# A decoder step on one core: expert turns dealt anew between the stages of a tile pair, and where their v rows are added up

## The chip, the cores and the metric

One core of a Trainium2 chip runs the whole kernel. The metric is device microseconds (us) of one execution. The engines are TensorE (PE in the profile, with its weight loads as PEld), VectorE (DVE), ScalarE (ACT), GpSimd (POOL) and SyncE (SP, which only issues transfers). Each engine runs its own program in order; they meet through semaphores.

## What is computed

One layer of a hybrid decoder over 1024 prompt tokens (8 tiles of 128 rows) and 8 sample tokens with a paged cache of 4096 positions each. Every token goes through latent attention and retention side by side, merged by sigmoid gates, and then through a product-key expert layer. Cut to what matters here:

```python
def merge_branches(o_lat, o_ret, rg, ga, gb, w_uv, ret_norm_g, w_oa, w_ob, w_out):
    o_a = einsum('bshc,chv->bshv', o_lat, w_uv).reshape(B, S, -1) @ w_oa
    o_b = (silu(rg) * head_group_norm(o_ret, ret_norm_g)) @ w_ob
    return (sigmoid(ga) * o_a + sigmoid(gb) * o_b) @ w_out

def peer_block(tb, w_q, sub_keys, expert_u, expert_v):      # 128 tokens
    q = rms(tb @ w_q)                                        # 8 heads x 2 halves x 128
    s = einsum('thpd,phkd->thpk', q, sub_keys)               # 128 keys per half
    sv, si = top_k(s, 16)
    eid, g = best 16 of the 16 x 16 sums, softmax of them    # per head
    act = gelu(einsum('thk d,td->thk', expert_u[eid], tb))
    return einsum('thk,thkd->td', g * act, expert_v[eid])
```

The expert layer dominates the traffic: each token picks 8 x 16 = 128 experts, and for each of these one row of 1024 floats is read from `expert_u` and one from `expert_v`. For one tile that is 128 u gathers and 128 v gathers, each of 128 partitions x 4 KB = 524,288 bytes.

## The kernel before

**Two strands.** The *front* of a tile is everything up to the choice of its experts; the *experts* are the gathers and what is done with them. The front of later tiles is computed while the experts of earlier tiles run. The experts are written as steps (L2498 on VectorE, L1339 on TensorE, L2603 on ScalarE): step s takes u row s (one VectorE instruction, L2507, a product with the token and a sum, into `dots`) and v row s - 20 (`LAG`). There are 8 x 128 + 20 = 1044 steps, and two steps make a *turn* (522 turns). GpSimd (L814) issues all gathers in that order, u and v by turns, into a ring of 9 row buffers (`RING`); a buffer comes free when its row is used.

**Where a v row is added up.** Either VectorE multiplies it by its coefficient and adds it into `xr` (L2535), or TensorE multiplies it by a diagonal of coefficients and adds it into PSUM (L1351: two matmuls of 128x512 floats, which the profile has as four records; ScalarE makes the diagonal first, L2629, three steps ahead, in 8 slots). The list `on_pe` (L504 to L507) says which: it looks up the name of the stage in which step n + 20 runs. Stages in `ALL_ON_PE` give all their v rows to TensorE, those in `MOST_ON_PE` two of three, those in `HALF_ON_PE` every second one, and all others none.

**Units.** The tiles go in five units: (0), (1, 2), (3, 4), (5, 6), (7). A unit of two, a pair, does attention and retention of its two tiles one after the other (the *tile stages*: lat, uq, reto, squares, normed, keys, 16 of head, ov for each), then the *output stages* for both at once, so that each weight block is read once and used for both: rg (8 loads), oa (4), gate (8), ob (8), gate (8), merge, out (8), x2, wq (16). A load is 512 KB into one of 4 slots of `wbuf`, issued by SyncE as slots come free; for a pair it feeds four matmuls of 128x512 (eight records). Last comes *choosing*: pqT (2), top (4), xT, linA (24 loads, which are the first weight blocks of the next lead tile and of the tile beside it) on TensorE, while VectorE picks the best keys and works out the ids (`choose` L2156, `dve_chosen` L2200). After the five units comes the sample part, with the paged cache.

**How the order is set.** Each engine's front is a generator that yields the name of its stage; all three yield the same names in the same order. `beside` (L843) takes the front up to a yield, then lets the experts run as many turns as the deal gives to that place, on each of the three engines:

```python
def dealt(names, total, weight):                       # L481
    for i, n in enumerate(names):
        so_far += weight(i, n)
        upto = int(total * so_far / whole + 0.5)
        deal.append(upto - given)
```

`total` is the unit's number of turns, `UNIT_TURNS` = (0, 64, 128, 128, 72), and the weights are `BESIDE` (L2709). The sample part has the other 130 turns, by `SAMPLE_SHARES`.

**Draining.** TensorE writes a block into one of four PSUM banks in turn (`A`, banks 0, 1, 2, 6); for a pair, two banks per block. ScalarE drains it (`act_block`, L1427): it yields once less than the block has loads, waits until the block is used up (`w_used`), drains both banks, then yields once more. `act_linA` (L1475) has the same form with 3 + 1 yields. On VectorE, `gated` and `gate` (L2054, L2073) apply the gates; where they stand among the yields is written out at L2097 to L2130. TensorE may refill a bank only after it was drained (`may_fill`), so a block waits for the drain of the one two before it.

Of the kernel before, what the change touches and what calls it, by code (L numbers as in the profile page):

```python
# [107 lines left out]
def program(nc, a, out, const):  # L108
    _, SEQ, D = a["x_prompt"].shape
    NB = a["x_sample"].shape[0]  # L110
    _, NPHYS, PAGE, KVL = a["cache_ckv"].shape
    ROPE = a["cache_krope"].shape[3]
    _, _, RH, RDK, RDV = a["state_ret"].shape
# [5 lines left out]
    _, _, PH, NK, PD = a["peer_sub_keys"].shape  # L119
# [73 lines left out]
    with ExitStack() as ctx:  # L193
# [1233 lines left out]
        def act_block(act, tiles, name, i, emit, ready=None):  # L1427

            for _ in range(load_at[tiles[0], name, i][1] - 1):
                yield name  # L1430
            if ready is not None:
                ready()
            act.wait_ge(w_used, used_through(tiles[0], name, i))
            for x, t in enumerate(tiles):
                emit(x, A.bank(t, name, i)).then_inc(A.drained, 1)
            yield name
# [38 lines left out]
        def act_linA(act, t):  # L1475
# [17 lines left out]
            for i in range(NA):  # L1493
                for _ in range(3):
                    yield "linA"
# [8 lines left out]
                yield "linA"  # L1504
# [543 lines left out]
        def dve_unit(dve, u):  # L2048
# [47 lines left out]
            for i in range(4):  # L2096
                yield "rg"  # L2097
            for x in range(2):
                gated(0, x)
                yield "rg"  # L2100
            yield "rg"
            yield "rg"
            for x in range(2):
                gated(1, x)
                yield "oa"
            yield "oa"
            yield "oa"
            for i in range(4):
                yield "gate"
# [3 lines left out]
            yield "gate"  # L2113
            yield "gate"
            for x in range(2):
                gate(1, x)
                yield "ob"
            for i in range(6):
                yield "ob"
            for i in range(4):  # L2120
                yield "gate"
# [3 lines left out]
            yield "gate"  # L2125
            yield "gate"
# [550 lines left out]
        def _(dve):  # L2677
# [31 lines left out]
BESIDE = {"lat": 1.5, "uq": 1.0, "reto": 1.5, "squares": 1.5, "normed": 1.5, "keys": 1.5, "head": 2.0, "ov": 1.5, "rg": 0.25, "oa": 0.25,  # L2709
          "gate": 0.25, "ob": 0.25, "merge": 2.0, "out": 0.25, "x2": 2.0, "wq": 0.3, "pqT": 1.0, "top": 1.0, "xT": 1.0, "linA": 0.4,  # L2710
          "end": 0.0}
ALL_ON_PE = ("lat", "uq", "reto", "squares", "normed", "keys", "ov", "merge", "x2", "pqT", "top", "xT")
MOST_ON_PE = ("head", "page")
HALF_ON_PE = ("ret",)
# [70 lines left out]
```

## Time and profile before

| | |
|---|---|
| runs of the kernel before | 4503.61 and 4514.61 us, median 4509.11 us |
| the profiled execution, its own time | 4466.19 us |
| its span | 4464.4 us |
| HBM read | 1404.99 MB |
| row gathers (software queue q0) | 1082.26 MB |
| mean granted TensorE clock | 0.871 |
| 1024 u gathers, 1024 v gathers on GpSimd | 1129.5 and 1242.3 us busy |
| VectorE: 1024 u rows (L2507), 422 v rows (L2535) | 1239.2 and 542.8 us busy |
| TensorE: 602 v rows (L1351, 2408 records) | 1320.7 us busy |

The profiled execution is one of its own, 42.9 us (1%) below the median of the runs. Busy time of TensorE is modelled: back to back, a record of 128x512 begins every 0.43 us, though its mean length is given as 0.6. GB/s in a window is all traffic of the core, and "DMA share" is how busy its 16 DMA engines were.

### The profile page before, as it was taken

Reading aid. Unit: us, or ns where it says so; the run is one execution under the profiler, and the core shown is the slowest. Engines: PE = TensorE matmul, PEld = TensorE weight load, DVE = VectorE, ACT = ScalarE, POOL = GpSimd, SP = SyncE. Lnnn points to the kernel's source line nnn. Section 1 sums busy time; section 2 is a strip of 40 time slices with the busy share of each in tenths; the row PEclk is TensorE's granted clock in tenths of the full one; section 3 lists DMA queues with packets and bytes.
Section 4 is the critical chain, followed back from the end, with each engine's and each line's share of the span. In section 5 each row is a group of like instructions: output and inputs, shape, how many; then the busy total and the mean of one; then the engine's idle time right before and its main releaser. Section 6 shows DMA issues by size and latency. Waiting matters only on the chain.

```text
span 4464.4 us, 38637 instructions
## 1 busy us (share of the span) xinstructions
PE 3261.3 (73%) x11093; PEld 1612.4 (36%) x11093; DVE 2729.5 (61%) x6242; ACT 725.0 (16%) x2211; POOL 2390.5 (54%) x2069
## 2 busy tenths in 40 slices
PE   7886889887686898866776988677773667778313
PEld 4343434433232344333333444233331335545211
DVE  2157633686666536976656446976548757676676
ACT  2112210211121112111121112121111111111101
POOL 0006732347777533557767434557536656566774
PEclk8997899998898999978898999888897789988556
DMA  5758986679999987989999977889998999999996
GB/s 172 242 187 307 357 289 220 237 256 375 363 379 363 358 283 274 330 294 349 365 371 356 334 270 278 323 320 350 371 350 303 327 346 345 369 364 350 393 398 256
DMA packets 541606, 1425.12 MB, mean 319 GB/s; under 512 B 88234, under 2 KB 147251, under 8 KB 541395
## 3 DMA queue, kind: packets, MB, share of 16 engines
q0 software_dynamic: 297216, 1082.26, 65.3%
q1 hardware_dynamic: 197666, 314.45, 20.5%
q10 hardware_dynamic: 46514, 25.96, 2.0%
q8 instruction: 90, 1.47, 0.1%
q14 instruction: 120, 0.98, 0.1%
HBM read 1404.99 MB, written 17.47 MB: 319 GB/s over the span
## 4 chain that ended last, share of the span: by engine, by line
PE 32%; POOL 20%; DVE 17%; issue 15%; DMA 11%; another core or an unknown queue 2%; ACT 2%; SPq 0%; ACTq 0%; DVEq 0%; POOLq 0%
POOL rows L820 20%; PE PS L884 18%; DMA rows<-in_peer_v_dram,pe_id 6%; PE PS L1351 6%; DVE rows L2507 3%; DVE xr L2535 3%; PE PS L941 2%; PE PS L864 1%; DMA out_ret_s_dram<-KV 1%; DMA rows<-in_peer_u_dram,pe_id 1%; DVE WK L2248 1%; DMA wbuf<-in_w_in_dram 1%; PE PS L1268 1%; DVE WK L2251 1%
## 5 line engine op out<-in xcount | busy, mean ns | idle before, releaser
L820 POOL DMA_INDIRECT rows<-in_peer_v_dram,pe_id x1024 | 1242.3, 1213 | 1182.9 <-DVE dots L2507 899.0
L1351 PE MATMUL PS<-rows,diags 128*128 128x512 f32 x2408 | 1320.7, 688 | 472.3 <-DMA rows<-in_peer_v_dram,pe_id 414.9
L2507 DVE CUSTOM_DVE_ANT_0 rows<-rows,px 128x1024 f32<-128x1024 f32 x1024 | 1239.2, 1221 | 573.2 <-DMA rows<-in_peer_u_dram,pe_id 528.8
L820 POOL DMA_INDIRECT rows<-in_peer_u_dram,pe_id x1024 | 1129.5, 1103 | 837.3 <-DVE pe_id L2255 290.8
L1351 PEld LDWEIGHTS PS<-rows,diags 128*128 128x128 f32 x2408 | 487.1, 217 | 1130.4 <-issue 1104.2
L2535 DVE SCALAR_TENSOR_TENSOR xr<-rows,gcoef,xr 128x1024 f32<-128x1024 f32 x422 | 542.8, 1286 | 89.0 <-issue 72.0
L884 PE MATMUL PS<-wbuf,xt 128*128 128x512 f32 x800 | 400.1, 609 | 30.0 <-DMA wbuf<-in_peer_w_q_dram 11.9
L884 PE MATMUL PS<-wbuf,z 128*128 128x512 f32 x752 | 384.9, 596 | 4.6 <-DMA wbuf<-in_w_oa_dram 2.6
L2629 ACT ACTIVATE diags<-ident,gcoef 128x128 f32<-128x128 f32 x602 | 209.7, 393 | 296.6 <-DVE gcoef L2524 143.4
L941 PE MATMUL PS<-wbuf,xt 128*128 128x512 f32 (+1 forms) x480 | 226.3, 569 | 22.3 <-DMA wbuf<-in_w_in_dram 9.8
L884 PE MATMUL PS<-wbuf,wide 128*128 128x512 f32 (+1 forms) x416 | 204.1, 602 | 33.1 <-ACT z L1451 10.4
L884 PEld LDWEIGHTS PS<-wbuf,xt 128*128 128x128 f32 x800 | 149.9, 194 | 213.1 <-issue 170.0
L884 PEld LDWEIGHTS PS<-wbuf,z 128*128 128x128 f32 x752 | 143.7, 191 | 187.6 <-issue 177.5
L864 PE MATMUL PS<-ident,WK 128*128 128x128 f32 x548 | 92.6, 313 | 145.0 <-DVE WK L2296 46.6
L864 PE MATMUL PS<-ident,z 128*128 128x128 f32 x133 | 24.5, 323 | 181.8 <-DVE z L1954 176.2
L864 PEld LDWEIGHTS PS<-ident,WK 128*128 128x128 f32 x548 | 78.6, 165 | 199.7 <-issue 51.5
L949 PE MATMUL PS<-wbuf,KV 128*128 128x512 f32 (+1 forms) x288 | 135.1, 551 | 0.0
L941 PEld LDWEIGHTS PS<-wbuf,xt 128*128 128x128 f32 x480 | 86.5, 194 | 117.2 <-issue 79.1
L884 PEld LDWEIGHTS PS<-wbuf,wide 128*128 128x128 f32 x416 | 80.1, 198 | 134.9 <-issue 89.5
L1024 PE MATMUL PS<-KV,qt 96*128 96x512 f32 (+3 forms) x192 | 89.6, 582 | 44.2 <-DVE mx L2032 32.5
L1045 PE MATMUL PS<-KV,WK 128*128 128x64 f32 x576 | 85.1, 296 | 47.5 <-issue 28.7
L1574 ACT ACTIVATE WK<-PS 128x512 f32<-128x512 f32 (+3 forms) x96 | 44.1, 489 | 400.3 <-PE PS L864 267.7
(417 smaller groups left out, 2937.0 us busy)
## 6 DMA issues: line engine op xcount, KB each, us to landing
wbuf<-in_w_in_dram SPq DMA_DIRECT2D x226, 512.0 KB
wbuf<-in_peer_w_q_dram SPq DMA_DIRECT2D x88, 512.0 KB
wbuf<-in_w_out_dram SPq DMA_DIRECT2D x44, 512.0 KB
wbuf<-in_w_ob_dram SPq DMA_DIRECT2D x42, 512.0 KB
KV<-in_cache_ckv_dram SPq DMA_DIRECT2D x144, 128.0 KB
rows<-in_peer_u_dram,pe_id POOLq DMA_INDIRECT x1028, 5.4
rows<-in_peer_v_dram,pe_id POOLq DMA_INDIRECT x1024
wbuf<-in_w_oa_dram SPq DMA_DIRECT2D x24, 512.0 KB
```

The lines of the kernel that those rows point to most:

```text
L820: pool.indirect_dma_start(row_slot(kind, n), None, a["peer_u" if kind == "u" else "peer_v"][0], bass.IndirectOffsetOnAxis(ap=pe_id[t % 3][ ...
L864: last = nc.tensor.transpose(b[0:m, k * n:(k + 1) * n], src, ident[0:n, 0:n])
L884: last = nc.tensor.matmul(b[:, 0:wd], lhs[x][:, (k0 + j) * P:(k0 + j + 1) * P], block_w[:, j * wd:(j + 1) * wd], start=(k0 + j == 0), stop ...
L941: last = nc.tensor.matmul(A.bank(t, "linA", i)[:, 0:wd], xt[:, (k0 + j) * P:(k0 + j + 1) * P], block_w[:, j * wd:(j + 1) * wd], start=(fir ...
L949: last = nc.tensor.matmul(other[:, 0:wd], next_lhs(t, k0 + j), block_w[:, j * wd:(j + 1) * wd], start=(first_k and j == 0), stop=(last_k a ...
L1024: last = nc.tensor.matmul(DJ.bank(t, "score", h)[:, i:i + w], qt[0:HD, h * P:(h + 1) * P], key_t[0:HD, h, i:i + w], start=True, stop=True)
L1045: last = nc.tensor.matmul(bank[6][:, h * VH:(h + 1) * VH], pt[:, k * P:(k + 1) * P], value[:, k, h * VH:(h + 1) * VH], start=(k == 0), sto ...
L1268: last = nc.tensor.matmul(PS[:, at_:at_ + P], qsc[b % 2][:, k * P:(k + 1) * P] if k < 8 else qsc_rope[b % 2], blocks_of[:, k] if k < 8 els ...
L1351: last = nc.tensor.matmul(bank[3 + 4 * c], diag(n), row_slot("v", n)[:, c * 512:(c + 1) * 512], start=start, stop=stop)
L2507: V.tensor_tensor_reduce(out=row, in0=row, in1=px[:, :], scale=1.0, scalar=0.0, op0=ALU.mult, op1=ALU.add, accum_out=dots[:, at_:at_ + 1]) ...
L2535: V.scalar_tensor_tensor(out=y[:, :], in0=row_slot("v", n), scalar=gcoef[:, g % 2 * TOPK + k:g % 2 * TOPK + k + 1], in1=y[:, :], op0=ALU.m ...
L2629: nc.scalar.activation(diag(n), ident[:, :], ACT.Copy, scale=gcoef[:, g % 2 * TOPK + k:g % 2 * TOPK + k + 1]).then_inc(diag_ready.sem, 1)
```

## The change

The turns stay the same in number for every unit (`UNIT_TURNS` is not touched), and the sample part keeps its deal. What changes is the split inside a unit, the engine of some v rows, and the place of some drains and gates:

1. New weights in `BESIDE`: less for the tile stages, more for the output stages and for pqT and top.
2. linA joins `ALL_ON_PE`; head moves from `MOST_ON_PE` (two of three v rows on TensorE) to `HALF_ON_PE`.
3. `act_block` and `act_linA` drain a block one yield later, that is, behind the turns dealt to the block's last load.
4. On VectorE `gated` and `gate` stand later by up to four yields, to match.

```diff
@@ act_block
-            for _ in range(load_at[tiles[0], name, i][1] - 1):
+            for _ in range(load_at[tiles[0], name, i][1]):
                 yield name
             if ready is not None:
                 ready()
             act.wait_ge(w_used, used_through(tiles[0], name, i))
             for x, t in enumerate(tiles):
                 emit(x, A.bank(t, name, i)).then_inc(A.drained, 1)
-            yield name
@@ act_linA
-                for _ in range(3):
+                for _ in range(4):
                     yield "linA"
...
-                yield "linA"
@@ dve_unit
-            for i in range(4):
+            for i in range(8):
                 yield "rg"
-            for x in range(2):
-                gated(0, x)
-                yield "rg"
-            yield "rg"
-            yield "rg"
-            for x in range(2):
-                gated(1, x)
-                yield "oa"
-            yield "oa"
-            yield "oa"
-            for i in range(4):
+            for i in range(2):
+                for x in range(2):
+                    gated(i, x)
+                    yield "oa"
+            for i in range(6):
                 yield "gate"
             for x in range(2):
                 gate(0, x)
                 yield "gate"
-            yield "gate"
-            yield "gate"
+            for i in range(2):
+                yield "ob"
             for x in range(2):
                 gate(1, x)
                 yield "ob"
+            for i in range(4):
+                yield "ob"
             for i in range(6):
-                yield "ob"
-            for i in range(4):
                 yield "gate"
             for x in range(2):
                 gate(2, x)
                 yield "gate"
-            yield "gate"
-            yield "gate"
@@ the tables
-BESIDE = {"lat": 1.5, "uq": 1.0, "reto": 1.5, "squares": 1.5, "normed": 1.5, "keys": 1.5, "head": 2.0, "ov": 1.5, "rg": 0.25, "oa": 0.25,
-          "gate": 0.25, "ob": 0.25, "merge": 2.0, "out": 0.25, "x2": 2.0, "wq": 0.3, "pqT": 1.0, "top": 1.0, "xT": 1.0, "linA": 0.4,
+BESIDE = {"lat": 1.0, "uq": 0.8, "reto": 1.2, "squares": 1.2, "normed": 1.2, "keys": 1.2, "head": 1.5, "ov": 1.0, "rg": 0.45, "oa": 0.45,
+          "gate": 0.45, "ob": 0.45, "merge": 2.5, "out": 0.5, "x2": 2.5, "wq": 0.45, "pqT": 2.0, "top": 1.5, "xT": 1.0, "linA": 0.45,
           "end": 0.0}
-ALL_ON_PE = ("lat", "uq", "reto", "squares", "normed", "keys", "ov", "merge", "x2", "pqT", "top", "xT")
-MOST_ON_PE = ("head", "page")
-HALF_ON_PE = ("ret",)
+ALL_ON_PE = ("lat", "uq", "reto", "squares", "normed", "keys", "ov", "merge", "x2", "pqT", "top", "xT", "linA")
+MOST_ON_PE = ("page",)
+HALF_ON_PE = ("ret", "head")
```

## Rows read from the trace of the kernel before

**Rows 1.** The page: busy time of each engine, then 40 slices.

```profile
PE 3261.3 (73%) x11093; PEld 1612.4 (36%) x11093; DVE 2729.5 (61%) x6242; ACT 725.0 (16%) x2211; POOL 2390.5 (54%) x2069
...
PE   7886889887686898866776988677773667778313
...
POOL 0006732347777533557767434557536656566774
...
DMA  5758986679999987989999977889998999999996
```

**Rows 2.** Busy time by window, stages in turn; the first line names columns.

```profile
core 0: us, PE busy (x) PEld busy (x) DVE busy (x) ACT busy (x) POOL busy (x), PEclk, DMA share, GB/s
340.30:593.00 252.70, 188.17 (x527) 96.16 (x528) 171.72 (x367) 61.55 (x180) 181.13 (x156) 0.84 0.93 340
593.00:842.20 249.20, 234.92 (x619) 109.76 (x618) 87.31 (x228) 40.18 (x122) 54.01 (x46) 0.98 0.69 236
842.20:970.30 128.10, 94.89 (x264) 46.81 (x263) 122.97 (x451) 19.03 (x61) 42.47 (x34) 0.88 0.69 237
970.30:1503.00 532.70, 386.98 (x986) 176.87 (x987) 332.93 (x641) 95.96 (x279) 396.92 (x355) 0.89 0.97 364
1503.00:1776.00 273.00, 249.82 (x645) 116.80 (x644) 128.79 (x284) 42.46 (x130) 102.98 (x90) 0.96 0.83 295
1776.00:1939.10 163.10, 109.79 (x295) 50.67 (x293) 156.43 (x504) 21.53 (x70) 81.89 (x68) 0.87 0.83 295
...
2919.60:3159.80 240.20, 186.27 (x556) 92.85 (x557) 152.07 (x285) 50.00 (x131) 167.62 (x156) 0.90 0.95 353
3159.80:3361.50 201.70, 149.20 (x353) 63.19 (x352) 99.09 (x209) 26.80 (x83) 84.99 (x73) 0.92 0.96 359
3361.50:3472.90 111.40, 26.63 (x60) 10.24 (x58) 99.80 (x274) 10.37 (x29) 73.38 (x60) 0.65 0.81 286
```

**Rows 3.** Waits in the second pair's tile stages (total, times, longest).

```profile
DVE rows L2507 <- DMA rows<-in_peer_u_dram,pe_id: 161.0, 117, 3.3
PE PS L1351 <- DMA rows<-in_peer_v_dram,pe_id: 107.6, 57, 5.2
```

**Rows 4.** Chain of waits, second pair's output stages: start, us, what.

```profile
1503.51 68.68 PE PS L884 x160
...
1577.47 56.91 PE PS L884 x128
...
1640.12 6.87 PE PS L1351 x16
```

**Rows 5.** VectorE's groups, 1829 to 1939 us, second pair's choosing.

```profile
L2535 DVE SCALAR_TENSOR_TENSOR xr<-rows,gcoef,xr 128x1024 f32<-128x1024 f32 x20 | 25.8, 1289 | 0.7 <-issue 0.6
L2507 DVE CUSTOM_DVE_ANT_0 rows<-rows,px 128x1024 f32<-128x1024 f32 x20 | 24.5, 1224 | 0.3
```

**Rows 6.** Busy time by window, choosing stages of two pairs (columns as before).

```profile
841.60:875.00 33.40, 20.54 (x74) 11.80 (x72) 31.34 (x154) 11.85 (x44) 12.53 (x11) 0.85 0.55 182
...
949.40:979.80 30.40, 9.95 (x27) 5.05 (x26) 29.26 (x64) 3.04 (x10) 11.81 (x8) 0.66 0.52 158
1775.30:1826.40 51.10, 34.30 (x106) 15.95 (x105) 48.18 (x213) 14.36 (x52) 26.16 (x22) 0.93 0.75 258
1826.40:1905.90 79.50, 76.18 (x193) 35.18 (x191) 76.88 (x237) 6.01 (x13) 45.18 (x38) 0.98 0.98 361
1905.90:1948.90 43.00, 9.67 (x23) 4.78 (x23) 41.69 (x82) 3.82 (x13) 16.35 (x13) 0.56 0.62 203
```

**Rows 7.** Weight-load waits of TensorE, second pair's choosing.

```profile
PEld PS L864 <- DVE z L1954: 33.7, 1, 33.7
```

**Rows 8.** GpSimd's groups, 1826.4 to 1934.5 us, second pair's choosing.

```profile
L820 POOL DMA_INDIRECT rows<-in_peer_v_dram,pe_id x23 | 31.7, 1376 | 44.0 <-DVE dots L2507 38.9 <-issue 5.1
```

**Rows 9.** GpSimd's groups, 1042.8 to 1237.6 us, heads of one tile.

```profile
L820 POOL DMA_INDIRECT rows<-in_peer_v_dram,pe_id x67 | 79.9, 1193 | 20.7 <-issue 20.1 <-DVE dots L2507 0.6
```

**Rows 10.** Waits in the second pair's output stages.

```profile
ACT WK L1421 <- PE PS L884: 87.5, 7, 23.1
```

## The prediction

> **What bounds the kernel now.** I read the page first, for which engine is full. None is: TensorE is busy for 73% of the span, the others less, but the DMA line stands at 9 in long stretches and falls to 7 or 8 between them, and there GpSimd falls to 3 or 4 [rows 1]. So the limit changes with the stage, and I cut the span into windows at each unit's stages [rows 2]: for each unit tile stages, output stages (rg to wq), choosing (pqT to linA). The reader is to see three patterns in the second pair. Tile stages: 532.7 us, DMA share 0.97, 364 GB/s, no engine over 75%. Output stages: 273.0 us, TensorE busy 249.8, DMA only 0.83 and 295 GB/s. Choosing: 163.1 us, VectorE busy 156.4, DMA again 0.83. The waits agree: in the tile stages VectorE and TensorE wait for rows to arrive, 161.0 and 107.6 us [rows 3]; in the output stages the chain is unbroken runs of weight matmuls, 160 records in 68.68 us [rows 4]. The rows are thus short of bandwidth in one stage while bandwidth lies idle in the two others.
>
> The deal before, by the formula: a pair's weights sum to 128.4, of which the two tiles have 90, so of 128 turns 90 lie in the tile stages, 21 in the output stages, 17 in choosing. After: 68 of 124.7, so 70, 36 and 22. The pair with 64 turns goes from 45, 11, 8 to 35, 18, 11; the single tile with 72 from 40, 17, 15 to 28, 26, 18. A turn moves four rows, 2.10 MB, which is 5.76 us at 364 GB/s.
>
> **Fewer turns in the tile stages.** They are bound by arriving rows, so a turn gone is its transfer gone: 20 x 5.76 = 115 us in the second pair, and the same in the third. The last tile: 12 turns at 353 GB/s, 5.94 us each, 71. The first pair's share is 0.93, not 0.97, so I take 50 of the 58 that 10 turns give. Sum -351. What is late next must stay below the rows: with half of the head rows on VectorE, a head turn costs it 2 x 1.22 + 1 x 1.29 = 3.7 us [rows 5] of 5.76, so VectorE is no bound; TensorE gets less work.
>
> **More turns in the output stages.** The second pair's output stages move 273 x 295 = 80.5 MB; 15 turns add 31.5. 112 MB at 361 GB/s (the rate of a window where TensorE runs at full pace, [rows 6]) is 310 us, 37 more than now. VectorE has room (128.8 of 273, plus some 65). TensorE gets one turn more at merge and one more at x2, 4 rows x 1.72 us (16 records took 6.87 us, [rows 4]) = 7 us, and it stands still while those rows arrive; since the bandwidth is counted already, I add only 3. So +40 for each of the two full pairs. Bounds: 7 us (all rows fit beside the matmuls) and 15 x 5.76 = 86 (nothing does). The first pair moves 58.8 + 14.7 MB, 204 us at 361, below its 249: +2. The last tile's output stages are at 0.96 already, so 9 turns cost 9 x 5.84 (359 GB/s) = +53. Sum +135.
>
> **Choosing.** Between the last wq block and linA TensorE needs 33.4 us with 3 turns and 51.1 with 7 [rows 6], 4.4 us a turn; 4 more make +18 in a full pair, 2 more +9 in the first. In linA, v rows leave VectorE: 20 x 1.289 = 25.8 us of the 109.8 in which it is nearly always busy [rows 5]. But what goes off it comes on TensorE: 76.2 us of linA matmuls [rows 6] and 22 rows x 1.72 = 38. Behind them stands what lies between choosing and the next tile's first block: of the 43.0 us there, 33.7 are TensorE's wait for the next tile's latents [rows 7], and 9 are left; I add 5 for making the latents and 3 for late rows. That is 131 us, against 79.5 + 43.0 = 122.5 now. VectorE was the bound; TensorE becomes it. So +9, not a gain, together +27 for a full pair (bounds: -10, if only VectorE's relief counts, and +50, if each of 5 more turns and each row waits for itself). First pair: 74.4 + 12 x 1.72 + 14 = 109 against 104.8, +4, so +13. The last tile has no linA matmuls, so its relief is real (VectorE 99.8 busy of 111.4, 20.7 off, 7.3 on), but 38 MB of traffic needs 106 us: -3. Sum 54 + 13 - 3 = +64.
>
> **Later drains and gates.** ScalarE now serves the turns behind a block's last load before it waits for that block, instead of waiting first. Queued behind its wait were diagonals and the tanh of the experts; they come sooner. What waits now is the bank: TensorE needs it for the block after next, 32 records or 13.75 us later. As long as ScalarE trails by less than that, the price is nothing; if it trails, it is one turn per block that has a turn behind it (below). A gain is bounded by gaps such as the 5.3 us between the two long matmul runs, 1572.2 to 1577.5 [rows 4]. I take 0. SyncE's and GpSimd's queues keep their order; only the turns between which weights are asked for differ.
>
> **Sum.** -351 + 135 + 64 = -152 us on the profiled execution's own 4466.2, which makes 4314. That execution lies 1% under the median of the runs, so the median comes to 4314 x 4509.1 / 4466.2 = 4356 us.
>
> A v gather takes GpSimd 1376 ns beside the full VectorE of choosing and 1193 ns in the heads [rows 8, 9], so something of VectorE's work may reach it; the v rows on VectorE go from 422 to 458. The Trainium skill, "SBUF — State Buffer", section "SBUF: two separate sides", has a rule against such a move: a VectorE instruction with two SBUF inputs and a GpSimd operation that reads SBUF hold one port pair in turn, each for its whole length. By that rule in full the gathers would wait for every added row, which is rival (d); the sum takes nothing for it.
>
> **Rivals.**
> (a) *All bandwidth gets used.* If every stage reached 364 GB/s, the second pair's 322.5 MB would take 886 us instead of 968.8 (-83), the third's the same, the last tile's 189 MB 520 instead of 553 (-33), and the first pair -50: -249, own time 4217, median 4258. For it: 361 GB/s beside full-pace matmuls [rows 6]. Against it: turns bunched at merge, x2, pqT and top, where TensorE stops.
> (b) *A moved turn costs its full price.* Output stages stretch by 5.76 us for every turn, as they would if blocks and rows can't overlap: 86 instead of 40 in each full pair, 40 instead of 2 in the first: -22 in all, 4444, median 4487. For it: the last tile's output stages are DMA-bound [rows 2]. Against it: in the full pairs 160 records hold 0.43 us each [rows 4] with 5 turns beside them, and the DMA share leaves 0.14 free.
> (c) *The drain falls behind and TensorE pays.* Its place is the bank wait before the next block but one; it decides once ScalarE trails TensorE by more than 13.75 us, because its tanh waits for a VectorE that waits for rows. Price on top of (b): 16 turns on 36 loads put one behind 4 to 5 of 10 blocks, 5.76 us each, 26 a full pair, 13 and 21 in the others, 86; and in linA matmuls and rows in series, 79.5 + 63 + 14 = 157 instead of 131 (+52 for two pairs, +14 in the first). -22 + 152 = +130, own 4596, median 4640: slower. For it: ScalarE's work is strictly in order, and rows arrive late where DMA is full. Against it: ScalarE now waits for TensorE (87.5 us in 7 waits, [rows 10]), so it has time in hand.
> (d) *VectorE's rows hold up the gathers.* 36 more rows x 1.289 = 46 us, all of it on the path: 4360, median 4403. Against it: GpSimd is busy for 397 of 533 us even in the tile stages [rows 2]. The rule of the Trainium skill quoted above would have it so for each of them.
>
> **Chances.** Forecast 0.50, (a) 0.14, (b) 0.19, (c) 0.10, (d) 0.07. The range is 4270 to 4480: it holds the forecast with most of its bounds (40 may be 7 or 60), (d), and parts of (a) and (b), and leaves (c) out. A change of 2%, 90 us, is about what a measurement of this kernel can tell; the line is at 4419. Faster by more: 0.45 from the forecast, 0.14, 0.05 from (d), 0.03 from (b), 0.67. Slower by more: most of (c), 0.08. Within: 0.25.
>
> **What would show it.** Right: the second pair's tile stages near 418 us, still at a DMA share of 0.96 or more; its output stages near 313 us at over 350 GB/s, with gaps between L884 runs; in choosing, TensorE busy for nearly all of linA, no L2535 there, and no wait of 30 us for the next tile's latents. The count of L2535 is 458, of L1351 2264. Wrong: tile stages that shrink by less than 4 us a turn with the DMA share falling (then the front, not the rows, sets them); output stages over 345 us, (b); waits of L884 for ScalarE over a few us each, (c); output stages at 273 us, more than half of (a).

## The result and the profile after

| | before | after |
|---|---|---|
| median of the runs, us | 4509.11 | 4259.67 (4254.52 to 4264.82) |
| ratio, 95% interval | 1 | 0.9447 [0.9377, 0.9517] |
| profiled execution, own time, us | 4466.19 | 4254.52 |
| its span, us | 4464.4 | 4252.7 |

The kernel became 5.5% faster. The forecast was 4356 us in a range of 4270 to 4480: the sign was right, the saving came out 96 us too small, and the measured time lies just below the range. Rival (a), in which every stage uses the bandwidth, had 4258.

The page of the changed kernel, to be laid beside [rows 1]: busy time, the DMA engines in 40 slices, and the two groups of v rows.

```profile
PE 3223.9 (76%) x10949; PEld 1589.4 (37%) x10949; DVE 2778.4 (65%) x6278; ACT 716.3 (17%) x2175; POOL 2441.1 (57%) x2069
...
DMA  5766987779999999999999999999999999999996
GB/s 176 232 209 238 346 308 271 261 256 351 372 372 360 402 370 342 330 326 364 364 376 372 376 374 325 330 367 376 390 358 349 352 331 367 353 365 361 401 402 228
...
L1351 PE MATMUL PS<-rows,diags 128*128 128x512 f32 x2264 | 1269.6, 700 | 450.7 <-DMA rows<-in_peer_v_dram,pe_id 393.9
...
L2525 DVE SCALAR_TENSOR_TENSOR xr<-rows,gcoef,xr 128x1024 f32<-128x1024 f32 x458 | 588.5, 1285 | 145.6 <-issue 119.8
```

The counts 2264 and 458 are those that the prediction named, so the deal came out as worked out there. (VectorE's lines stand 10 lower now: v rows L2525, dots L2497.) The DMA line no longer falls to 7 and 8 behind the first pair: it is 9 until the last slice. What the digits hide is in the line under it: the rate still swings from 325 to 402 GB/s while the digit stays 9.

The windows by stage, as [rows 2]: first pair (tile stages, output stages), second pair (tile, output, choosing), last tile (the same three). The ends of stages in this and later tables were read to within some 4 us.

```profile
341.20:553.00 211.80, 158.19 (x446) 86.81 (x447) 150.89 (x328) 55.03 (x159) 136.43 (x118) 0.76 0.87 318
553.00:807.30 254.30, 234.53 (x619) 109.42 (x618) 116.80 (x267) 40.28 (x123) 85.01 (x72) 0.97 0.79 280
951.60:1370.50 418.90, 302.36 (x793) 145.55 (x794) 285.50 (x534) 80.88 (x228) 303.41 (x276) 0.81 0.96 360
1370.50:1656.70 286.20, 263.60 (x663) 117.77 (x662) 199.16 (x382) 43.07 (x133) 192.89 (x142) 0.96 1.01 383
1656.70:1851.70 195.00, 164.18 (x414) 73.21 (x412) 153.37 (x528) 31.93 (x103) 109.00 (x96) 0.96 0.88 314
2744.60:2912.90 168.30, 135.89 (x447) 72.67 (x448) 122.74 (x232) 41.92 (x104) 120.17 (x108) 0.88 0.97 360
2912.90:3145.80 232.90, 159.91 (x353) 65.03 (x351) 144.09 (x268) 27.60 (x85) 139.88 (x109) 0.91 1.01 389
3145.80:3257.60 111.80, 73.23 (x152) 26.74 (x150) 88.94 (x274) 18.02 (x50) 86.88 (x70) 0.91 0.89 323
```

Subtracting [rows 2], and doing the same for the third pair (420.5, 287.8 and 184.6 us now, against 542.3, 274.0 and 164.2), gives every term of the sum. All in us of the profiled executions.

| term | forecast | measured |
|---|---|---|
| tile stages (first, second, third pair, last tile) | -50, -115, -115, -71 = -351 | -41, -114, -122, -72 = -348 |
| output stages | +2, +40, +40, +53 = +135 | +5, +13, +14, +31 = +64 |
| choosing | +13, +27, +27, -3 = +64 | +16, +32, +20, 0 = +69 |
| start and sample part | 0 | +5 |
| sum | -152 | -212 |

One term is off, by half: the output stages. The sum of -212 is also somewhat small beside the medians, which differ by 249: before's profiled execution lay 1% under its runs' median, the changed kernel's only 0.1% under its own. The forecast carried before's 1% over to the changed kernel. So of the 96 us that it missed, 60 lie in the sum, and 36 in this step from the profiled execution to the median. The ratio is the better measure, and two more chips gave 0.9439 and 0.9438 (below).

A closer look at the second pair, windows again: a stretch of output stages between two waits, then from the last wq block to linA, linA, and from there to the next tile's first block.

```profile
1372.00:1510.00 138.00, 132.14 (x301) 54.77 (x300) 95.67 (x139) 16.91 (x43) 97.86 (x68) 0.98 1.04 401
1655.80:1736.40 80.60, 54.18 (x139) 22.52 (x138) 69.75 (x265) 20.09 (x70) 55.59 (x48) 0.92 0.87 310
1736.40:1846.70 110.30, 110.30 (x278) 50.99 (x277) 81.01 (x246) 11.35 (x31) 53.12 (x47) 1.00 0.89 312
1846.70:1861.00 14.30, 9.81 (x27) 4.63 (x26) 12.68 (x38) 3.05 (x10) 5.70 (x7) 0.88 1.00 357
```

In the first line TensorE is busy for 96% of the time and the DMA engines move 401 GB/s beside it. The prediction had 361 GB/s as the ceiling [rows 6]. The page of the kernel before already had two slices above that, 393 and 398 GB/s in the sample part, where weight loads run beside the rows (the third and second from the end):

```profile
GB/s 172 242 187 307 357 289 220 237 256 375 363 379 363 358 283 274 330 294 349 365 371 356 334 270 278 323 320 350 371 350 303 327 346 345 369 364 350 393 398 256
```

In the third line of the windows TensorE is busy all the time and VectorE is not: linA's bound has passed from the one to the other, as forecast.

The chain of waits of the second pair's output stages, which was unbroken matmuls before [rows 4]:

```profile
1371.15 24.26 PE PS L884 x56
1395.42 11.27 DMA wbuf<-in_w_oa_dram
...
1414.19 12.58 DMA wbuf<-in_w_in_dram
```

And the waits of the same stretch (total, times, longest):

```profile
ACT WK L1421 <- PE PS L884: 86.9, 7, 16.8
POOL rows L820 <- DVE dots L2497: 49.4, 8, 18.6
...
PEld PS L884 <- DMA wbuf<-in_w_in_dram: 17.0, 18, 2.2
```

Some weight loads now land late, by 2.2 us at most and 17.0 us in all for the loads of `w_in`, where the stage before had no such wait; part of this is hidden behind running matmuls. The chain draws such a load at its full length of 11 us, though TensorE stood still for 1.4 us at most. TensorE's busy time in this stage by line, v rows (L1351) before and after, then the blocks (L884) before and after:

```profile
1503.00:1776.00 273.00, 25.93 (x50) 10.46 (x48) 0.96 0.83 295
1370.50:1656.70 286.20, 33.23 (x66) 13.35 (x64) 0.96 1.01 383
...
1503.00:1776.00 273.00, 210.92 (x480) 90.60 (x480) 0.96 0.83 295
1370.50:1656.70 286.20, 217.77 (x480) 89.35 (x480) 0.96 1.01 383
```

The stage grew by 13.2 us. The four more v rows on TensorE took 7.3 us, which the prediction had priced at 7, though its sum took only 3. The same 480 records of the blocks took 6.9 us more: about what the traffic of 15 turns cost them. ScalarE waits for TensorE as before [rows 10], so it has not fallen behind.

### The profile page after: what moved, and what is told of

Read it like the earlier page. It is cut to its first block, busy times and chain, and to the rows that moved or that the text cites. A ratio compares the mean times of both kernels' runs of the same rounds, so it can differ in the third digit from the quotient of the medians.

```text
span 4252.7 us, 38318 instructions
## 1 busy us (share of the span) xinstructions
PE 3223.9 (76%) x10949; PEld 1589.4 (37%) x10949; DVE 2778.4 (65%) x6278; ACT 716.3 (17%) x2175; POOL 2441.1 (57%) x2069
## 4 chain that ended last, share of the span: by engine, by line
PE 39%; DMA 17%; POOL 17%; issue 12%; DVE 10%; ACT 3%; another core or an unknown queue 2%; ACTq 0%; SPq 0%; DVEq 0%; POOLq 0%
POOL rows L820 17%; PE PS L884 15%; PE PS L1351 10%; DMA rows<-in_peer_v_dram,pe_id 8%; PE PS L941 4%; DMA wbuf<-in_w_in_dram 4%; DVE rows L2497 3%; PE PS L949 2%; PE PS L864 1%; DMA wbuf<-in_peer_w_q_dram 1%; DMA rows<-in_peer_u_dram,pe_id 1%; DVE xr L2525 1%; DMA out_ret_s_dram<-KV 1%; PE PS L1268 1%
## 5 line engine op out<-in xcount | busy, mean ns | idle before, releaser
L820 POOL DMA_INDIRECT rows<-in_peer_v_dram,pe_id x1024 | 1256.2, 1227 | 845.2 <-DVE dots L2497 554.1
L820 POOL DMA_INDIRECT rows<-in_peer_u_dram,pe_id x1024 | 1165.6, 1138 | 912.9 <-DVE pe_id L2245 291.7
L1351 PE MATMUL PS<-rows,diags 128*128 128x512 f32 x2264 | 1269.6, 700 | 450.7 <-DMA rows<-in_peer_v_dram,pe_id 393.9
L2497 DVE CUSTOM_DVE_ANT_0 rows<-rows,px 128x1024 f32<-128x1024 f32 x1024 | 1237.9, 1221 | 453.5 <-DMA rows<-in_peer_u_dram,pe_id 396.5
L1351 PEld LDWEIGHTS PS<-rows,diags 128*128 128x128 f32 x2264 | 460.0, 218 | 1064.4 <-issue 1014.9
L2525 DVE SCALAR_TENSOR_TENSOR xr<-rows,gcoef,xr 128x1024 f32<-128x1024 f32 x458 | 588.5, 1285 | 145.6 <-issue 119.8
L884 PE MATMUL PS<-wbuf,xt 128*128 128x512 f32 x800 | 409.0, 618 | 53.5 <-DMA wbuf<-in_w_in_dram 29.7
L884 PE MATMUL PS<-wbuf,z 128*128 128x512 f32 x752 | 386.3, 598 | 7.5 <-DMA wbuf<-in_w_oa_dram 5.7
L2619 ACT ACTIVATE diags<-ident,gcoef 128x128 f32<-128x128 f32 x566 | 200.8, 395 | 312.8 <-DVE gcoef L2514 153.1
L884 PEld LDWEIGHTS PS<-wbuf,xt 128*128 128x128 f32 x800 | 147.3, 195 | 253.2 <-issue 144.5
L884 PE MATMUL PS<-wbuf,wide 128*128 128x512 f32 (+1 forms) x416 | 204.3, 604 | 32.2 <-ACT z L1450 10.4
L884 PEld LDWEIGHTS PS<-wbuf,z 128*128 128x128 f32 x752 | 144.2, 192 | 192.4 <-issue 178.4
L949 PE MATMUL PS<-wbuf,KV 128*128 128x512 f32 (+1 forms) x288 | 134.5, 549 | 0.0
L884 PEld LDWEIGHTS PS<-wbuf,wide 128*128 128x128 f32 x416 | 80.0, 198 | 132.6 <-issue 85.5
L1045 PEld LDWEIGHTS PS<-KV,WK 128*128 128x128 f32 x576 | 79.5, 214 | 53.9 <-issue 27.3
```

The source lines that it names most:

```text
L820: pool.indirect_dma_start(row_slot(kind, n), None, a["peer_u" if kind == "u" else "peer_v"][0], bass.IndirectOffsetOnAxis(ap=pe_id[t % 3][ ...
L884: last = nc.tensor.matmul(b[:, 0:wd], lhs[x][:, (k0 + j) * P:(k0 + j + 1) * P], block_w[:, j * wd:(j + 1) * wd], start=(k0 + j == 0), stop ...
L949: last = nc.tensor.matmul(other[:, 0:wd], next_lhs(t, k0 + j), block_w[:, j * wd:(j + 1) * wd], start=(first_k and j == 0), stop=(last_k a ...
L1045: last = nc.tensor.matmul(bank[6][:, h * VH:(h + 1) * VH], pt[:, k * P:(k + 1) * P], value[:, k, h * VH:(h + 1) * VH], start=(k == 0), sto ...
L1351: last = nc.tensor.matmul(bank[3 + 4 * c], diag(n), row_slot("v", n)[:, c * 512:(c + 1) * 512], start=start, stop=stop)
L2497: V.tensor_tensor_reduce(out=row, in0=row, in1=px[:, :], scale=1.0, scalar=0.0, op0=ALU.mult, op1=ALU.add, accum_out=dots[:, at_:at_ + 1]) ...
```

## The experiments

Each ratio is to the kernel before, run on the same chip. Chips differ (the kernel before took 4420 to 4482 us on them), so ratios of different chips are compared with care, and medians not at all.

### The parts alone (one chip, kernel before 4476.86 us)

**Only the deal**: `BESIDE` of the changed kernel, everything else as before.

> The kernel before with only the new weights of the deal; v rows stay where they were (two of three head rows on TensorE, linA rows on VectorE), drains and gates stand where they stood. Theory T (the gain is bandwidth that lay idle in the output stages and is now used by moved turns): nearly all of the gain, 0.950 to 0.962 of the kernel before, second pair's tile stages near 420 us, its output stages at over 375 GB/s and under 292 us. Rival D (the later drains and gates are what lets the turns ride along): output stages over 310 us, ratio 0.975 or more. Rival V (the engine of the v rows matters as much): ratio 0.97 or more, with choosing the stage that is longer.

**Only the later drains and gates**: the three hunks in `act_block`, linA's drain and the gates.

> The kernel before with only the drains and gates one turn further on. Theory T: 0.997 to 1.003 of the kernel before. Rival D: 0.99 or less, from shorter output stages (under 268 us in the second pair).

**Only the lists of v rows**:

```diff
-ALL_ON_PE = (..., "xT")
-MOST_ON_PE = ("head", "page")
-HALF_ON_PE = ("ret",)
+ALL_ON_PE = (..., "xT", "linA")
+MOST_ON_PE = ("page",)
+HALF_ON_PE = ("ret", "head")
```

> The kernel before with only the new lists of stages: linA rows all on TensorE, head rows split evenly. Theory T: within 0.994 to 1.004 of the kernel before; linA goes from 109.8 us, bound by VectorE, to 105 to 112, bound by TensorE; the tile stages stay at 530 us, since arriving rows set them. Rival V: 0.985 or less.

**The changed kernel with the drains and gates of before**:

> The changed kernel with drains and gates back in their old places. Theory T: within 0.5% of the changed kernel, so 0.944 to 0.955 of the kernel before. Rival D: 0.97 or more, with ScalarE waiting for TensorE ahead of the turns' diagonals and output stages over 300 us in the second pair.

| | median, us | ratio |
|---|---|---|
| only the deal | 4288.49 | 0.9573 [0.9543, 0.9602] |
| only drains and gates | 4484.06 | 1.0013 [0.9995, 1.0032] |
| only the lists | 4449.09 | 0.9931 [0.9910, 0.9952] |
| changed, old drains | 4252.09 | 0.9493 [0.9466, 0.9520] |

The deal brings 4.3%, the lists 0.7% alone and 0.8% on top of the deal, the drains alone nothing. (The last row leaves the changed kernel's ratio, 0.944 to 0.945 on three other chips, by 0.5%; a comparison on one chip follows below.) The deal's own windows (second pair's tile, output and choosing stages, last tile's choosing):

```profile
943.00:1368.40 425.40, 311.24 (x861) 151.61 (x862) 264.29 (x517) 86.26 (x245) 318.13 (x276) 0.88 0.95 355
1368.40:1655.50 287.10, 262.44 (x663) 117.84 (x662) 197.14 (x382) 42.99 (x133) 177.70 (x142) 0.96 1.00 383
1655.50:1852.30 196.80, 129.80 (x326) 56.70 (x324) 179.52 (x550) 25.24 (x81) 114.72 (x96) 0.87 0.88 315
...
3155.00:3289.50 134.50, 37.80 (x92) 15.16 (x92) 112.93 (x306) 15.55 (x47) 87.88 (x72) 0.70 0.82 297
```

The output stages are at 383 GB/s here too, so neither the lists nor the drains made that rate. Against the run with only the drains, on the same chip, the deal takes 367 us from the tile stages and adds 60 to the output stages and 91 to choosing. That last number is 31 more than in the changed kernel with old drains on the same chip: with linA's v rows on VectorE, it is busy for 179.5 of 196.8 us, and the last tile's choosing takes 134.5 us instead of 116.2. The lists give that back. In the run of the lists alone the second pair's choosing, and the last tile's, are

```profile
1783.80:1948.70 164.90, 144.03 (x374) 65.92 (x372) 132.56 (x484) 27.58 (x90) 79.71 (x68) 0.95 0.83 290
...
3360.90:3464.90 104.00, 63.19 (x140) 23.65 (x140) 85.40 (x284) 19.77 (x58) 72.63 (x61) 0.94 0.87 316
```

against 164.2 and 119.2 us in the run of the drains alone: nothing in the second pair, where TensorE takes over as the bound, and 15 us in the last tile, which has no linA matmuls. The third pair's choosing became 10 us shorter (154.6 against 164.9), which the second pair's did not.

### The engines of the v rows, and the number of row buffers (another chip, kernel before 4419.92 us)

**The changed kernel once more**, as the measure for the next three:

> The changed kernel itself, as the measure of the other runs of this group. Both theories: 0.948 to 0.951 of the kernel before.

**Head rows two thirds on TensorE again**: "head" back in `MOST_ON_PE`.

> The changed kernel with the head rows two of three on TensorE again (linA rows stay on TensorE). Theory T (heads are bound by arriving rows whichever engine adds them up): within 0.3% of the changed kernel, tile stages of the second pair 415 to 425 us. Rival V (the even split relieves TensorE on the path): 0.5 to 1% slower than the changed kernel.

**linA's rows split evenly**: "linA" from `ALL_ON_PE` to `HALF_ON_PE`.

> The changed kernel with every second linA row on VectorE again. Theory T (TensorE alone sets linA now, 110.3 of 110.3 us busy, with 19 us in rows that could go to VectorE at 81 of 110): linA in the second pair 94 to 100 us, the whole 0.5 to 1% faster than the changed kernel. Rival: VectorE's order of work holds it (its ids must be ready first), linA at 105 us or more and no gain.

**One row buffer fewer**: `RING = 8` instead of 9.

> The changed kernel with 8 row buffers instead of 9. Theory E (the DMA engines are full in the tile stages): tile stages of the second pair longer by under 2%, 360 GB/s kept. Rival Q (the ring of buffers, so the number of rows under way, limits the tile stages, and this is why they stop at 360 GB/s when the output stages reach 383): tile stages longer by 5 to 12%, under 345 GB/s.

| | median, us | ratio |
|---|---|---|
| changed kernel | 4173.04 | 0.9439 [0.9403, 0.9476] |
| head rows mostly on TensorE | 4193.37 | 0.9492 [0.9453, 0.9530] |
| linA's rows split | 4162.48 | 0.9398 [0.9362, 0.9434] |
| 8 buffers (one round) | 4269.48 | 0.9650 [0.9598, 0.9703] |

Taking head rows off VectorE again made the kernel 0.5% slower by the medians, and not faster: rival (d) is wrong. The intervals of the ratios overlap, but the fastest of its four runs (4189.12 us) is above the slowest of the changed kernel's four (4185.05). The prediction had given the even split nothing. Where the gain lies is not shown: the second pair's tile stages took 414.4 us here against 403.5, but 414.7 with linA's rows split, where the heads are as in the changed kernel:

```profile
936.20:1350.90 414.70, 299.12 (x792) 144.43 (x793) 285.87 (x534) 80.32 (x228) 307.06 (x276) 0.81 0.97 363
```

So this stage differs by 11 us between executions without any change to its own turns. Splitting linA's rows shortened the two full pairs' choosing by 11 and 5 us and the first pair's by 10, and cost the last tile 6. In the whole time that is 0.25% by the medians and 0.4% by the ratios, with runs and intervals that overlap, where 0.5 to 1% was expected: no gain is shown for the kernel. In the stage itself both extremes are too much for linA in a pair, a bound on VectorE and one on TensorE.

With 8 buffers the second pair's tile and output stages are

```profile
959.20:1385.20 426.00, 303.56 (x793) 146.80 (x794) 285.72 (x534) 80.36 (x228) 308.39 (x277) 0.82 0.95 355
1385.20:1672.20 287.00, 260.88 (x662) 116.70 (x661) 198.98 (x382) 43.11 (x133) 190.40 (x141) 0.98 1.00 380
```

and with 9, on the same chip,

```profile
944.00:1347.50 403.50, 296.94 (x791) 143.32 (x792) 285.13 (x534) 80.33 (x228) 293.84 (x276) 0.82 0.98 374
1347.50:1635.00 287.50, 263.61 (x665) 117.74 (x664) 198.61 (x382) 43.08 (x133) 171.93 (x142) 0.97 1.00 382
```

The tile stages lose 22 us, the output stages none. Since the second pair's tile stages vary by 11 us, the third pair's are the better witness: 426.9 us with 8 buffers, 405.4, 406.8 and 407.4 in the three kernels with 9. The rate of the tile stages therefore depends on how many rows are under way, and is no ceiling of the memory, although the DMA share stands at 0.95 to 0.98 beside it. It isn't set by the buffers alone: 11% fewer of them took 4 to 5% off the rate, to 355 and 360 GB/s in the two pairs, where the theory of the buffers had expected under 345.

### Weight loads beside rows where there were none (one look)

If rows alone can't fill the DMA engines, loads in another queue should raise the traffic. This kernel issues 24 extra loads of weights during the heads of each unit's last tile (six rounds over the first four weight buffers, which nobody reads until the real loads):

```diff
+            for rep in range(6):
+                for n in range(first, first + WSLOTS):
...
+                    sp.dma_start(w_place(n)..., w[...]).then_inc(again, 16)
```

> The changed kernel with 24 more weight loads of 512 KB (12.6 MB) in each unit, issued by SyncE into the four weight slots before the first real rg loads, two and two, while the heads of the unit's last tile run; they hold the same data as the real ones. Theory Q (the DMA engines have time left when only row gathers are under way, and transfers of another queue use it): in the second pair's last 26 head turns, now about 54 MB in 150 us or 360 GB/s, the traffic rises to 380 GB/s or more, and those heads take 165 to 175 us. Theory E (360 to 374 GB/s is what the core can read in that stage): GB/s stays within 2% of the stage without the loads and the heads take 185 us.

Its one execution took 4348.88 us, beside 4481.48 for the kernel before. The extra loads, in the timeline:

```profile
1232.31 86.76 SPq L685 DMA_DIRECT2D wbuf<-in_w_in_dram  x24
```

Windows in the heads of the same pair without them, with them, and behind them, then all of the 26 head turns:

```profile
1059.00:1145.00 86.00, 57.10 (x130) 26.34 (x130) 59.42 (x99) 14.58 (x38) 62.50 (x60) 0.74 0.96 365
1232.00:1333.00 101.00, 57.31 (x146) 26.70 (x145) 52.15 (x90) 14.98 (x38) 60.66 (x54) 0.76 1.03 400
1340.00:1420.00 80.00, 50.07 (x132) 23.70 (x133) 50.74 (x82) 10.53 (x29) 55.97 (x52) 0.83 0.99 370
1243.10:1420.00 176.90, 105.03 (x260) 49.09 (x261) 104.58 (x169) 22.30 (x62) 114.37 (x101) 0.78 1.01 387
```

365, 400, 370 GB/s: the traffic rises by 8 to 10% with the second queue and falls when it ends. (The last four loads of the unit are issued at 1333 us; behind them, from 1380 us, it is 343 GB/s.) It is not free for the rows: 12.6 of the 40.4 MB in the middle window are weights, so rows came at 275 GB/s there. The 26 head turns took 176.9 us, where the changed kernel has 153.7 at 364 GB/s, on another chip. The 12.6 MB would be 35 us at that rate and cost 23. That lies between the two theories: the rate of 387 passes the 380 of the one, the time misses its 165 to 175 us by 2.

### How far the deal can go

**More turns still in the output stages**:

```diff
-BESIDE = {... "head": 1.5,  ... "rg": 0.45, "oa": 0.45, "gate": 0.45, "ob": 0.45, ... "out": 0.5,  ...
+BESIDE = {... "head": 1.27, ... "rg": 0.65, "oa": 0.65, "gate": 0.65, "ob": 0.65, ... "out": 0.65, ...
```

That makes 62, 44 and 22 turns of a pair instead of 70, 36 and 22.

> The changed kernel with the deal pushed on: 8 more turns of a full pair from the heads (70 to 62) into the output stages (36 to 44). Theory T: the output stages are full at 383 GB/s now, so (109.6 + 16.8) MB need 330 us instead of 286, as much as the tile stages give back (46 us): within 0.5% of the changed kernel, 0.940 to 0.950 of the kernel before. Rival (turns still ride for about 1 us each as the first 15 did): output stages under 300 us, ratio 0.93 or less.

**More turns in linA, split evenly**: linA 0.7, pqT 1.5, top 1.2, the blocks 0.5.

> The changed kernel with every second linA row on VectorE and the deal moved once more: in a full pair 3 turns fewer in the tile stages and 3 fewer between wq and linA, 6 more in linA. Theory T (each stage at its own bound): between wq and linA 58 to 63 us instead of 77, linA 105 to 115 instead of 92, tile stages 17 us shorter; 0.930 to 0.938 of the kernel before. Rival (VectorE holds linA, since choosing the ids is its own work): linA over 125 us, ratio 0.94 or more.

On one chip (kernel before 4481.48 us): 4204.96 us, 0.9381 [0.9353, 0.9409], and 4242.47 us, 0.9453 [0.9421, 0.9486]. The first is a small gain over the changed kernel's 0.944 of other chips, the second none, although 0.930 to 0.938 was expected of it. In the first the pairs' output stages (first pair, second pair) read

```profile
517.90:777.90 260.00, 239.34 (x621) 110.97 (x620) 141.85 (x303) 40.90 (x125) 108.26 (x92) 0.96 0.87 316
...
1292.10:1618.50 326.40, 258.54 (x655) 117.29 (x654) 240.74 (x437) 42.71 (x132) 225.81 (x173) 0.91 1.01 390
```

Against the changed kernel's 286 to 289 us on three other chips, 8 more turns cost the second pair some 39 (330 us was expected), 5 each: this stage is full near 390 GB/s, and past it a turn pays nearly its price. That is the mean of a flat stretch and a slower one; four windows of 40 us from its start read 400, 402, 404 and 402 GB/s. In the first pair 4 more turns cost nothing; there was still room, at 316 GB/s.

The second kernel shows that the count of turns isn't all. It has 36 turns in the output stages of a pair, as the changed kernel has, and yet they took 303.3 and 302.9 us. The second pair's, in two parts, and then the changed kernel's:

```profile
1341.30:1500.00 158.70, 147.80 (x346) 63.14 (x346) 111.24 (x163) 21.40 (x52) 112.64 (x81) 0.98 1.03 401
1500.00:1644.60 144.60, 118.89 (x321) 56.27 (x321) 86.61 (x211) 22.41 (x82) 72.65 (x65) 0.91 0.87 322
...
1370.50:1530.00 159.50, 150.19 (x349) 63.65 (x348) 108.50 (x163) 22.35 (x56) 109.22 (x78) 0.97 1.01 388
1530.00:1656.70 126.70, 113.41 (x315) 54.12 (x314) 90.67 (x220) 20.73 (x77) 83.67 (x65) 0.96 1.00 377
```

The loss is in the second part, at 322 GB/s, where TensorE once waits 8.6 us for a drain by ScalarE (L1657), the kind of wait that rival (c) had in mind. That the turns' places among the loads did this is likely, but no run took it apart.

**The room of the first pair used** (another chip, kernel before 4423.35 us). The weights of the kernel above, others for the first pair, which come to 27, 27 and 10 turns, and linA's rows split evenly except in the last tile:

```diff
+FIRST_PAIR = {"rg": 1.1, "oa": 1.1, "gate": 1.1, "ob": 1.1, "out": 0.9, "wq": 0.6}
...
-        deals = [dealt(names, UNIT_TURNS[u], lambda i, n: BESIDE[n]) ...
+        deals = [dealt(names, UNIT_TURNS[u], lambda i, n: FIRST_PAIR.get(n, BESIDE[n]) if u == 1 else BESIDE[n]) ...
```

> The deal pushed on (44 turns of a full pair in the output stages), in the first pair further (27, 26, 11 instead of 35, 18, 11), and every second linA row on VectorE in the three pairs, all of them on TensorE in the last tile, which has no linA matmuls. Theory T: the first pair's tile stages lose 8 turns or 46 us against the changed kernel and its output stages, at 280 GB/s there, grow by under 10; linA 95 instead of 110 us in a full pair; in all 60 to 85 us, 1.4 to 2.0%, faster than the changed kernel. Rival: the front of the first pair (two tiles' attention) sets its tile stages once few turns are left, under 20 us gained there, and the whole at most 1.2% faster.

and, on the same chip, the changed kernel, and the changed kernel with the old drains:

> The changed kernel once more, as the measure on this chip. Theory T and rival D alike: 0.943 to 0.952 of the kernel before.

> The changed kernel with drains and gates in their old places, beside the changed kernel on one chip. Theory T (the later drains are worth nothing, the missing 60 us of the output stages are bandwidth): within 0.3% of the changed kernel. Rival D (the later drains give part of it, because ScalarE no longer holds up turns dealt to a block's last load): 0.4 to 0.8% slower than the changed kernel, output stages 5 us or more longer in each full pair.

| | median, us | ratio |
|---|---|---|
| first pair's room used | 4084.48 | 0.9234 [0.9203, 0.9264] |
| changed kernel | 4177.23 | 0.9438 [0.9415, 0.9461] |
| changed, old drains | 4172.65 | 0.9436 [0.9413, 0.9458] |

The later drains and gates are worth nothing here as well. The first is 2.2% faster than the changed kernel, a little more than was expected (1.4 to 2.0%). Its first pair (tile, output, choosing), then the second's:

```profile
347.40:496.80 149.40, 117.19 (x397) 68.56 (x396) 112.19 (x268) 50.94 (x145) 98.32 (x84) 0.85 0.87 322
496.80:756.20 259.40, 241.28 (x628) 109.53 (x627) 168.07 (x335) 40.70 (x125) 149.34 (x112) 0.98 0.95 360
756.20:886.70 130.50, 113.08 (x298) 52.60 (x296) 121.08 (x455) 21.61 (x70) 50.13 (x40) 0.93 0.76 262
886.70:1241.30 354.60, 272.94 (x760) 132.93 (x761) 255.18 (x489) 77.28 (x219) 265.59 (x245) 0.85 0.98 376
1241.30:1567.30 326.00, 260.07 (x656) 117.59 (x655) 240.67 (x437) 42.74 (x132) 229.08 (x173) 0.91 1.01 390
```

and the changed kernel's first pair on that chip:

```profile
339.10:540.60 201.50, 148.05 (x441) 82.03 (x442) 146.42 (x321) 55.00 (x159) 134.86 (x117) 0.80 0.88 327
540.60:798.60 258.00, 238.21 (x627) 111.03 (x626) 121.62 (x276) 40.58 (x124) 87.47 (x75) 0.97 0.80 282
798.60:942.60 144.00, 121.81 (x326) 57.15 (x324) 117.85 (x455) 23.52 (x77) 51.99 (x46) 0.95 0.75 256
```

Nine more turns (36 rows) beside the first pair's blocks cost 1.4 us, at 360 instead of 282 GB/s, and the tile stages are 52.1 us shorter: 64 of some 94 us of the gain lie in this one pair. The rest is mostly the second's. This chip also gives the price of 8 more turns in the two full pairs' output stages without a change of chip: 36.7 and 45.2 us, 4.6 and 5.7 a turn.

## Why the prediction was wrong, step by step

- **The deal and the tile stages**: right. 70, 36 and 22 turns, the counts of v rows, and a turn at its full transfer: 20 turns fewer took 114 and 122 us (115 forecast), 418.9 us against "near 418". The DMA share stayed at 0.96, so the rows kept setting these stages. Taken as the deal alone on one chip, all tile stages gave 367 us, where 351 were forecast. The first pair gave 41 of the 50 that its share of 0.93 had been taken for.
- **The output stages: the step that failed**, a term mis-sized. "112 MB at 361 GB/s is 310 us" took a rate for the ceiling that was only the rate of one window. The stage ran at 383 GB/s and took 286.2 us; the last tile's ran at 389, where 9 turns had been charged at 359. 64 us instead of 135. The 361 came from linA, in which VectorE was busy for 76.88 of 79.50 us [rows 6]: the row itself says that an engine could have held the rows back there. The 364 of the tile stages was no ceiling either, as the 8 buffers and the added loads showed. The lower bound of 7 us, all rows beside the matmuls, was the nearer end: a moved turn cost 13.2 / 15 = 0.9 us, and half of that was TensorE's own v rows. With 64 in place of 135 the forecast would have been 4284 us, 24 us over the measured median and inside the range; the step from the profiled execution to the median, worth 36 us, took it out.
- **Its bounds**: the range reached to 4270 because the chance given to the lower bound was small; the rival that held the measured case had 0.14. What should have spoken for it is that no rate near 360 had been tested. In linA an engine could have held it. In the tile stages there was hardly anything beside the rows. The strongest case for a ceiling was the last tile's output stages, 359 GB/s at a share of 0.96 with no engine full [rows 2], and the change took just that stage to 389. And before's own page had slices at 393 and 398.
- **Choosing**: right in sum, 69 against 64, with two errors that cancelled. From wq to linA a turn cost 29.5 / 4 = 7.4 us, not 4.4 (VectorE is busy for 69.75 of 80.6 us there; no run shows the cause); linA with what follows took 124.6 us, 2 more than before, where 9 were added and 131 forecast. That VectorE's bound passes to TensorE was right: busy for all of linA, and the 33.7 us wait for the latents [rows 7] is down to 4.7, with 14.3 us between linA and the next tile's first block where 43.0 were.
- **Later drains and gates**: 0, right, in two comparisons on one chip each: alone (1.0013) and in the changed kernel (0.9438 with them, 0.9436 without).
- **(a) All bandwidth gets used**: nearest in time (0.944 against 4258 / 4509 = 0.944), and right that idle bandwidth in the output stages gets used, but its size is partly luck. By the profiled executions it asked for 38 us more than came. Not every stage reached its 364 GB/s: the first pair's stood at 318 and 280, the second's choosing at 314, while the output stages behind the first pair went to 380 to 389. The errors went opposite ways.
- **(b) A moved turn costs its full price**: wrong for this change (13 us, not 86), and nearly right for the next 8 turns, at some 5 us each. Both ends of the bound were true, one after the other; the step between them lies between 36 and 44 turns, where the stage's mean goes from 383 to 390 GB/s.
- **(c) The drain falls behind**: wrong for this change. ScalarE's waits for TensorE are 86.9 us in 7 [rows 10 had 87.5], so its time in hand was not touched, and no wait of L884 for ScalarE is over 3.7 us. Another place of the turns brought one of 8.6 us (above).
- **(d) VectorE's rows hold up the gathers**: wrong. 36 more rows on VectorE, the total came out lower, and fewer of them in the heads did not help. The rule of the Trainium skill, "SBUF — State Buffer", section "SBUF: two separate sides", may still hold for the single instruction (a v gather took 1376 ns beside a full VectorE and 1193 ns in the heads, [rows 8, 9]), but GpSimd, busy for 303 of 419 us in the tile stages, had the time to bear it. No run here took the two apart further.

What stays open: whether the 400 to 404 GB/s of the fullest windows are the memory's limit or that of the queues; why the even split of head rows gains 0.5%, and in which stage; why 36 turns in other places took 303 us instead of 287; and what an even split of the head rows does to TensorE's clock (below) and that to the time.

## What to carry to other kernels

Read a rate as a ceiling only in a window where nothing else could have held it, and best where two queues were busy: here stages of almost only rows stood at 355 to 378 GB/s, and the same rows with weights beside them at 380 to 401. Deal background work by what each stage has idle, unit by unit: one table of weights for units of 64 and of 128 turns left the first at 282 GB/s. And price a moved piece twice, below the point where the receiving stage is full and above it (0.9 and 5 us a turn here). Before a difference of one stage is called an effect, look at the same stage in a run that left it alone: here that alone gave 11 us.

## What was not expected of the hardware

- The DMA share goes over 1 (1.04 at 401 GB/s, 1.03 at 400), and 0.95 to 0.98 stands beside anything from 355 to 376 GB/s. It says that something is under way, not that nothing more fits.
- The tile stages of the second and third pair, nearly all gathers of rows, moved 355 and 360 GB/s with 8 buffers, and 374 and 375 with 9 on the same chip.
- The rate of the tile stages differs by chip: in the third pair 362 GB/s on the first chip and 357 on the second (with old drains), but 375 and 378 on two others. That of the second pair's output stages hardly differs (380 to 383).
- 15 turns (60 rows of 0.52 MB) beside 273 us of output stages lengthened them by only 5%.
- With the head rows split evenly, TensorE's granted clock in the second pair's tile stages is 0.81 of full speed (a mean over stretches at 2.4 GHz and at 1.2) where it was 0.89 [rows 2], and with them two thirds on TensorE it is 0.89 again (window 950.00 to 1364.40 of that run): TensorE has less to do there and runs slower. No effect on the stage's time is shown: at 0.82 and 0.81 it took 403.5 and 414.7 us, at 0.89 414.4.
